# Residual block with conv and MLA mixing on one core: the opening's order of work on TensorE and VectorE, and when the modulation ring's first loads go out

## The reference, cut to what matters

```python
mod = (silu(c) @ ada_w + ada_b).reshape(b, 9, 1024)         # ada_w: 1024 x 9216
h = rmsnorm(x, norm_ffn1_g) * (1 + sc1) + sh1               # mod 1 is the scale, mod 0 the shift
x = x + 0.5 * g1 * ((silu(h @ w1) * (h @ w3)) @ w2)         # w1, w3: 1024 x 2816
h = rmsnorm(x, norm_mix_g) * (1 + sc2) + sh2
x = x + g2 * (concat(conv_mixer(h @ w_in), mla(h @ w_in)) @ w_out)
x = x + 0.5 * g3 * swiglu(rmsnorm(x, norm_ffn2_g) * (1 + sc3) + sh3, ...)
return rmsnorm(x, final_norm_g)
```

## Time and profile before

| | us |
|---|---|
| median of 3 runs | 1001.19 |
| lowest, highest | 999.53, 1002.65 |
| the profiled execution's own time | 1003.0 |
| its span, first to last instruction | 1001.3 |
| PE busy | 984.2 (98%) |
| VectorE (DVE) busy | 550.2 (55%) |
| ScalarE (ACT) busy | 350.0 (35%) |

### The profile page before, as it was taken

The page is one execution under the profiler, slowest core; times in us unless marked ns, Lnnn a source line. Parts: engine busy times, 40 slices in busy tenths (PEclk is TensorE's granted clock), DMA queues, the critical chain, the costliest instruction groups (busy, mean ns, idle before and its releaser), DMA issues.

```text
span 1001.3 us, 13134 instructions
## 1 busy us (share of the span) xinstructions
PE 984.2 (98%) x4515; PEld 807.5 (81%) x4515; DVE 550.2 (55%) x772; ACT 350.0 (35%) x542; POOL 52.1 (5%) x79
## 2 busy tenths in 40 slices
PE   7999999999999999999999999999999999999997
PEld 3678888888888888888888888888888888888886
DVE  3757877687666445845376539754334344333332
ACT  4243232323242332542255634532323323323222
POOL 2011111111000000000000320000000000000000
PEclk9999999999999999999999999999999999999999
DMA  9758766786553333223221212233332333333232
GB/s 327 248 154 266 251 194 206 229 257 200 170 157 108 92 93 106 78 81 99 84 69 43 86 43 88 82 105 92 97 103 85 105 88 100 99 96 97 81 111 84
DMA packets 180637, 128.93 MB, mean 129 GB/s; under 512 B 5392, under 2 KB 168018, under 8 KB 180608
## 3 DMA queue, kind: packets, MB, share of 16 engines
q1 hardware_dynamic: 172064, 98.71, 32.9%
q0 software_dynamic: 8400, 29.58, 8.9%
q10 hardware_dynamic: 144, 0.26, 0.1%
HBM read 126.44 MB, written 2.10 MB: 128 GB/s over the span
## 4 chain that ended last, share of the span: by engine, by line
PE 92%; DVE 3%; DMA 2%; ACT 2%; issue 1%; SPq 0%; DVEq 0%; ACTq 0%
PE pb L868 86%; PE pb L1040 1%; DMA ada_start<-in_ada_w_dram 1%; DMA raw<-in_ffn_w_dram 1%; DVE wl L1407 1%; PE pb L909 1%; PE pb L1014 1%; ACT wh L440 1%; DVE ubuf L1446 0%; PE pb L891 0%; PE pb L1031 0%; PE pb L1210 0%; PE pb L1387 0%; DVE hl L1439 0%; DVE acc L1633 0%
## 5 line engine op out<-in xcount | busy, mean ns | idle before, releaser
L868 PE MATMUL pb<-hh,wh 128*128 128x512 f32 x880 | 345.8, 393 | 2.7 <-DVE sbuf L1504 1.1
L868 PE MATMUL pb<-hh,wl 128*128 128x512 f32 x880 | 342.7, 389 | 0.0
L868 PE MATMUL pb<-hl,wh 128*128 128x512 f32 x880 | 342.5, 389 | 0.0
L1407 DVE TENSOR_TENSOR wl<-raw,wh 128x1024 fp32r<-128x1024 f32 x156 | 191.1, 1225 | 238.3 <-ACT wh L440 238.0
L440 ACT ACTIVATE wh<-raw 128x1024 fp32r<-128x1024 f32 x159 | 168.4, 1059 | 437.5 <-PE pb L868 429.0
L868 PEld LDWEIGHTS pb<-hh,wh 128*128 128x128 f32 x880 | 165.2, 188 | 39.3 <-DVE wl L1407 2.1
L868 PEld LDWEIGHTS pb<-hh,wl 128*128 128x128 f32 x880 | 165.2, 188 | 34.8
L868 PEld LDWEIGHTS pb<-hl,wh 128*128 128x128 f32 x880 | 165.3, 188 | 33.0
L868 PE MATMUL pb<-gh,wh 128*128 128x512 f32 x368 | 143.4, 390 | 0.0
L868 PE MATMUL pb<-gh,wl 128*128 128x512 f32 x368 | 143.2, 389 | 0.0
L868 PE MATMUL pb<-gl,wh 128*128 128x512 f32 x368 | 143.2, 389 | 0.0
(11 more groups left out here) (257 smaller groups left out, 716.2 us busy)
## 6 DMA issues: line engine op xcount, KB each, us to landing
raw<-in_ffn_w_dram SPq DMA_DIRECT2D x102, 512.0 KB, 3.7
ada_ring<-in_ada_w_dram POOLq DMA_DIRECT2D x56, 512.0 KB, 5.3
raw<-in_ffn_w_dram SPq DMA_DIRECT2D x32, 448.0 KB, 3.4
raw<-in_w_in_dram SPq DMA_DIRECT2D x17, 512.0 KB, 3.7
ada_start<-in_ada_w_dram SPq DMA_DIRECT2D x16, 512.0 KB, 9.2
raw<-in_w_out_dram SPq DMA_DIRECT2D x8, 512.0 KB, 3.4
x_nat<-in_x_dram SPq DMA_DIRECT2D x4, 512.0 KB, 5.1
out_dram<-o_nat SPq DMA_DIRECT2D x3, 512.0 KB, 3.4
```

Of the source, the lines that this page charges most:

```text
L868: last = pe.matmul(o, a, b, start=start and j == 0 and t == 0, stop=stop and j == len(pairs) - 1 and t == 2)
L1407: dve.tensor_tensor(wl[par][:, :], raw[par][:, :], wh[par][:, :].bitcast(F32), ALU.subtract).then_inc(lo_ready, 1)
```

## The change

The order of work in the opening is changed on SP, POOL, ACT, PE and DVE, and the ring's start is split in two. `raw_first` moves to slots 2 and 3 of the ring.

- PE: the transposes of the small vectors, the spread of the norm and the last two transposes of `x` stand among the rows of group 0, before `start_sum(0)`. The rows of group 1 stand one by one between the plain products of tile 0, which begin right after `start_sum(0)`.
- ACT: all eight copies of `x` come ahead of the first row copy.
- DVE: the copies of the small vectors come ahead of the chunks; `start_mod(0)` and two `plain_u` come ahead of group 1's chunks; chunks of groups 2 and 3 alternate with `plain_u` and `shifted_lo`.
- SP: one DMA of group 2 goes ahead of `raw_first[1]`, and unit 2's load ahead of the last two DMAs of group 3.
- POOL: the first two ring loads wait for the last shift values (`mods_ready`) alone. The third waits for `bias_done` and for the VectorE split of unit 5.

```diff
-        (raw_first,), _ = place(region + 2 * FT * 4 * SEQ, ("raw_first", [P, 2, UW], F32))
+        (raw_first,), _ = place(region + 2 * FT * 4 * SEQ + 2 * 4 * D_MODEL, ("raw_first", [P, 2, UW], F32))
@@ sync
             start_load(1)
+            start_load(2, (0,))
             sp.dma_start(raw_first[:, 1, :] ...).then_inc(first_landed[1], 16)
-            start_load(2)
-            start_load(3)
+            start_load(2, (1, 2, 3))
+            start_load(3, (0, 1))
             load(U_A1 + 2, 0, w1v[0][:, :, P:2 * P])
+            start_load(3, (2, 3))
             load(U_A1 + 3, 1, w3v[0][:, :, P:2 * P])
@@ gpsimd
-            pool.wait_ge(bias_done, 1)
+            pool.wait_ge(mods_ready, 2)
             with pool.Fori(0, N_MOD - 2) as j:
                 for k in range(DT):
+                    if k == 2:
+                        pool.wait_ge(bias_done, 1)
+                        pool.wait_ge(lo_ready, U_A1 + 6)
                     pool.wait_ge(ada_step, ADA_START + j * DT + k - 3)
@@ scalar
-            for k in range(DT - 2):
+            for k in range(DT):
                 copy_x(k)
             row_copy(0)
-            copy_x(DT - 2)
-            copy_x(DT - 1)
             row_copy(1)
@@ tensor
-            pe.wait_ge(siluc_ready, 1)
-            start_rows(0, ADA_ON_PE[0])
-            turn_last(DT - 2)
-            turn_last(DT - 1)
             ... (transposes of vec1 and vec2, as before)
+            pe.wait_ge(siluc_ready, 1)
+            start_rows(0, (0,))
+            pe.wait_ge(vec_ready, 3)
+            norm_spread(N_FFN1)
+            turn_last(DT - 2)
+            start_rows(0, (2,))
+            turn_last(DT - 1)
+            start_rows(0, (4, 6))
             pe.wait_ge(consts_landed, 16)
             start_sum(0)
-            pe.wait_ge(vec_ready, 3)
-            norm_spread(N_FFN1)
-            pe.wait_ge(x_copied, 3)
-            start_rows(1, ADA_ON_PE[1])
             pe.wait_ge(x_copied, 6)
             plain_steps(0, (0,))
+            start_rows(1, (0,))
+            plain_steps(0, (1,))
+            start_rows(1, (2,))
+            plain_steps(0, (2,))
+            start_rows(1, (4,))
+            start_rows(1, (6,))
+            plain_steps(0, (3,))
             start_sum(1)
-            plain_steps(0, (1, 2, 3))
             plain_steps(1, range(HALF))
@@ vector
-            for k in ADA_ON_DVE[0]:
-                start_chunk(0, k)
             dve.wait_ge(vec_turned, 2)
             ... (two copies into vcol, as before)
+            for k in ADA_ON_DVE[0]:
+                start_chunk(0, k)
+            start_mod(0)
+            plain_u(0)
+            plain_u(1)
             start_chunk(1, 1)
-            start_mod(0)
             start_chunk(1, 3)
-            plain_u(0)
+            plain_u(2)
             start_chunk(1, 5)
-            plain_u(1)
+            plain_u(3)
             start_chunk(1, 7)
-            plain_u(2)
-            plain_u(3)
             start_chunk(2, 0)
             start_chunk(2, 1)
+            start_chunk(2, 2)
+            start_chunk(2, 3)
             start_mod(1)
             for k in range(HALF, DT):
                 plain_u(k)
-            for k in range(2, DT):
                 start_chunk(2, k)
-            for k in range(3):
-                start_chunk(3, k)
+            start_chunk(3, 0)
+            start_chunk(3, 1)
             start_mod(2)
+            start_chunk(3, 2)
+            shifted_lo(0)
             start_chunk(3, 3)
-            shifted_lo(0)
             split_lo(U_A1 + 2, 0)
             for k in range(1, HALF):
                 shifted_lo(k)
+                start_chunk(3, 3 + k)
             split_lo(U_A1 + 3, 1)
-            for k in range(HALF, DT):
-                start_chunk(3, k)
+            start_chunk(3, DT - 1)
             start_mod(3)
```

More of the change, by code:

```diff
@@ L304, in _, with start_load @@
                 sp.dma_start(x_nat[:, t, :], x[0][t * P:(t + 1) * P, :]).then_inc(x_landed[t], 16)
-            def start_load(g):
+            def start_load(g, pieces=range(4)):
                 v, half = divmod(g, 2)
                 col = (D_MODEL if v == 0 else 0) + half * HALF_COLS
-                for i in range(4):
+                for i in pieces:
                     sp.dma_start(ada_start[:, DT * v + 2 * i:DT * v + 2 * i + 2, half * HALF_COLS:(half + 1) * HALF_COLS],
@@ L1009, in start_rows @@
             def start_rows(g, ks):
-                v, half = divmod(g, 2)
                 for k in ks:
                     pe.wait_ge(start_landed[g][k // 2], 16)
-                    ins = pe.matmul(pb[ROW_BANK[g]][0:1, :], silu_c[:, k:k + 1],
-                                    ada_start[:, DT * v + k, half * HALF_COLS:(half + 1) * HALF_COLS],
+                    ins = pe.matmul(pb[ROW_BANK[g]][0:1, :], silu_c[:, k:k + 1], ada_start[:, k, g * HALF_COLS:(g + 1) * HALF_COLS],
                                     start=k == ADA_ON_PE[g][0], stop=k == ADA_ON_PE[g][-1])
```

## The result

The changed kernel takes 1003.85 us (median of 20 runs, 1001.94 to 1006.90), the kernel before 1001.63 in the same count. The ratio is 1.0025, 95% interval 1.0016 to 1.0035: slower by 2.5 us (by 2.2 between the two medians). That is just under the 0.3% that I had named as the least that can be told, and outside my range (997.8 to 1002.6). The profiled execution took 1005.97, its span is 1004.3.

What follows compares the result with a forecast made beforehand. PE, busy 98% of the span, was taken as the bound. Opening plus 0.5 and ring minus 1.2 gave minus 0.7: 1002.3 us profiled, 1000.5 against the median, range 997.8 to 1002.6.

Steps and rivals of the forecast that it cites:

- The clock: Opening: the one fall to half clock stays, from 20.7 to 23.7 us, costing 1.5 instead of 1.7: minus 0.2 us.
- Rival 2: Clock falls once more around 47 to 52 us, or idle from 16.8 draws the fall out: 1.7 us; chance 0.10.
- Spread gone from behind the sum: Behind the first sum: PE idles about 1.2 us, first plain product at 20.7, 0.15 us later.
- Rows among the plain products: From 20.7 us on: seven switches between rows and plain products priced at 0, bounds 0 to 1.1 us.
- Vectors, spread and turns among the rows: Group 0's rows: moved work fills pauses, last row 0.4 us later, start_sum(0) still at 17.5; gives nothing.
- Chunks in turn: Second steps start at 42.6, new 0.5 us wait for unit 3, second half at 52.1; opening plus 0.5.
- SP's order: Opening loads: reordered loads still land in time, hidden by 2 us or more; cost 0.
- Ring: Near 71 us: unit 6's load takes 3.7 us instead of 9.29, PE's 1.12 idle goes: minus 1.2 us.

Runs made afterwards that it cites:

- after_again: The changed kernel as it is, measured again on the same chip as other variants: median 1005.63 us, ratio 1.0025 to the kernel before.
- turns_only: The kernel before with only VectorE's turned chunks (from group 2 on) and SP's new order: 1002.21 us, ratio 0.9997.
- after_filled: The changed kernel plus three wide matmuls nobody reads, one ahead of start_sum(0) and two behind it: 1002.37 us, ratio 1.0003 to the kernel before.
- early_only: The kernel before with only the vectors, spread and turns among group 0's rows, and the copies reordered: 1001.74 us, ratio 0.9990.
- after_together: The changed kernel with group 1's four rows together between plain products 0 and 1 of tile 0: 1003.00 us, ratio 1.0009 to the kernel before.
- after_rows_first: The changed kernel with group 1's rows together right behind start_sum(0), ahead of the plain products: 1000.15 us, ratio 0.9981 to the kernel before.
- among_only: The kernel before with only group 1's rows among the plain products and plain_u(0) and (1) ahead of chunks: 1007.52 us, ratio 1.0042.
- early_ring: The kernel before with vectors, spread and turns among group 0's rows, plus the ring part: 999.58 us, ratio 0.9978.
- ring_only: The kernel before with the ring part alone (raw_first at slots 2 and 3, ring loads in two steps): 1001.99 us, ratio 0.9985.
- after_no_among: The changed kernel with group 1's rows together ahead of the first plain product and VectorE's order there as before: 1000.64 us, ratio 0.9993.

## Why the prediction was wrong

The forecast was minus 0.7: minus 0.5 of PE's order and the ring, and minus 0.2 for the clock. after_again has plus 0.8 and plus 1.8. Two steps failed: the clock's term is off by 2.0 us, and PE's order by 1.3, for the two terms of the pause and of the alternation.

**The clock (forecast minus 0.2).** This is the larger of the two failures. I kept one fall at nearly its full price and gave a further one 0.10. Measured, the clock costs the changed kernel 1.8 us more on average than the kernel before (5.44 against 3.60), about the price of one more fall. Rival 2's mechanism and price were right. Of its two places one was wrong (33 us, not 47 to 52), and the other, the idle that draws the first fall out, is what after_again's profile shows: 0.58 from 20 to 24 us and 0.50 from 24 to 27. I had used to argue that an emptier stretch keeps the fall, and did not ask whether it makes falls more frequent; one profile shows only one outcome (turns_only's has none at 20 us). The Trainium skill ("TensorE: Matmul & The Clock Gate", on the clock gate) says that recent activity of PE releases the half rate; after_filled agrees, with 3.4 us less cost from wide products in the pauses.

**Spread gone from behind the sum (forecast plus 0.15).** I had the pause (1.2 us, measured 1.33) but let it be paid for by the spread's 1.14. That holds only if the first sum starts at 17.5. It started at 18.53 in the profiled execution, 17.95 in early_only. I let PE work without a break from 11.0 on, but it waited for group 0's first data until 11.88. PE's first row starts anywhere from 10.88 to 12.27 in the profiles, so a part of this is scatter. Rows beside narrow products took 0.95 to 1.02 us, not 0.86. So the first plain product came at 21.86 instead of 20.7. after_together less after_rows_first puts 0.93 on the pause and what went with it.

**Rows among the plain products (forecast 0, bounds 0 to 1.1).** The bounds held in the changed kernel and the value taken was wrong. Five of the seven changes cost 0.73, near the upper end that I had worked out from the lone pair of 1.02 us. An unbroken run of one kind of product says nothing about alternation. The bounds also left out that `start_sum(1)` moves behind the plain products, and with it VectorE's `start_mod(1)`. Alone (among_only) this part cost 3.7.

**Vectors, spread and turns among the rows (forecast 0).** Alone minus 0.6, because the rows could follow the sum at once. Beside the ring part it shows nothing (early_ring). In the change there was a wait for VectorE in place of the lead.

**Chunks in turn (forecast plus 0.5)** measured plus 0.65 ± 0.25, with the new wait for unit 3 that I had forecast at 0.5 (0.37 idle at 51.58). **SP's order** cost nothing that a row shows. **Ring (forecast minus 1.2)** measured minus 1.2; unit 6's load fell from 9.29 to 3.8 us. The Trainium skill ("DMA: Bandwidth & Descriptors", on queues, rings and completion order) says that a DMA engine serves in turn, packet by packet, the queue rows it has work for. I had read this as equal shares, by which the ring's loads would not be what delays unit 6. That reading doesn't fit: without them beside it the load took 3.7 us in ring_only.

The loss splits so: all parts but the rows among the plain products minus 0.9 at full clock (after_no_among), these plus 1.6, the clock plus 1.8. With the rows together again the clock costs 3.08 ± 0.49, as in the kernel before, so both losses come with that part. This is a split and no check, since the 1.6 is the difference of two kernels; but after_rows_first, which puts the rows together in another place, comes out alike (996.24 and 996.30). What stays open is why the clock falls again at 33 us, and what decides the late falls.

## What to carry to other kernels

When independent short work is moved ahead to fill pauses, look at what it covered where it stood: here the spread hid VectorE's way to the first plain product, and the rows, which needed nothing, were moved behind the very product that had to wait. A time at 98% busy on PE is still exposed to its clock: a stretch of one-column products and pauses costs more than its own length, and one profile shows one outcome of it, so judge by several runs' clocks, and look in the profile for where all the falls are. Price each side of an interleave by the lone pair, not by the unbroken run.

## What was not expected of the hardware

One program's runs differ in how long the clock is down: the kernel before ran at mean clocks from 0.994 to 1.000, most of them at 0.994, 0.996 or 0.998, which is some 2 us from one to the next, near the 1.7 of a fall. Three useless wide matmuls in a thin stretch lowered the mean cost of the clock from 5.44 ± 0.61 to 2.00 ± 0.46 us. With one of 512 columns it went from 2.41 ± 0.43 to 1.41 ± 0.19 in one kernel and stayed in another (2.27 ± 0.38 and 2.17 ± 0.60). And a slow start of PE need not show in the granted clock: in after_filled's profile a pair of matmul records took 1.86 us instead of 1.02 at a clock that reads 1.00.
